# RG-LRU and the front of HGRN2 moved from the mixer tiles into the projection pass of a hybrid encoder layer

## The chip, the cores and the metric

One Trainium2 chip, one core of it. The time is that of one execution of the whole program on the device, in microseconds; the median of three runs is given. The kernel is written at the level of engines: TensorE (PE), VectorE (DVE), ScalarE (ACT), GpSimd (POOL) and SyncE (SP) each run a program of their own in order, and wait for each other on semaphores.

## The reference

One layer, for two groups of tokens that share the weights: a prompt of 2048 and a sample of 32. `D_MODEL` is 1024. A projection to 6536 columns feeds four mixers of width 512; their outputs are gated, joined (2048) and projected back; then comes cross-attention into 256 memory tokens.

```python
h = rms_norm(x, g_pre[l])
p = jnp.matmul(h, w_in[l]).astype(f32)
xa, ga, pb, gb, xbc, dtr, z, qd, fd, idd, gd = split_last(p, SPLITS)
# RG-LRU
xa_c, nca = causal_conv(xa, conv_a[l], lru_conv_w[l], lru_conv_b[l])
...
r = jax.nn.sigmoid(jnp.einsum('btnd,nde->btne', xb, w_r).reshape(Bsz, T, C) + b_r)
i = jax.nn.sigmoid(jnp.einsum('btnd,nde->btne', xb, w_i).reshape(Bsz, T, C) + b_i)
log_a = -LRU_C * r * jax.nn.softplus(-lam)
a = jnp.exp(log_a)
u = jnp.sqrt(-jnp.expm1(2.0 * log_a)) * (i * x)
...
_, h = lax.associative_scan(combine, (a, u), axis=1)
...
ya = ya * jax.nn.silu(ga)
# HGRN2, in chunks of 64
logf = jnp.logaddexp(jnp.log(lb), jnp.log1p(-lb) + jax.nn.log_sigmoid(fd))
...
k = -jnp.expm1(logf)
b = jnp.cumsum(lfc, axis=1)
o = jnp.einsum('blhk,bhkv->blhv', qc * jnp.exp(b), S)
dec = jnp.exp(jnp.where(mask, b[:, :, None] - b[:, None, :], -jnp.inf))
att = jnp.einsum('bthk,bshk,btshk->btsh', qc, kc, dec)
```

With `DEPTH` = 1 the lower bound `lb` is 0, so `logf` is the log-sigmoid of `fd`. The other two mixers are RWKV-7 and Mamba-2 SSD.

## The kernel before

The program is a row of passes, each a block of five engine programs.

`project_pass` normalises and transposes x (one tile of 128 tokens after the other), and then computes the projection, transposed: channels on partitions, tokens (2048 + 32 = 2080) along the free axis. A unit is 128 channels; there are 52 units, in the order of the list `units`, and each has five groups of N = 416 columns. A group is 24 matmuls in a PSUM bank (three per 128 rows of `D_MODEL`, from the split of float32 into a high and a low part). The five groups use banks 0 to 4, so a bank is wanted again five groups later; TensorE waits for that on `bank_free`. Per group ScalarE and VectorE take the bank over: a gate is `tanh` and a product (`silu`), a convolution is ScalarE's column of the newest tap and three taps on VectorE (`own_column`, `older_columns`), a shift is one tap, the rest a copy (`plain`). A unit's 2080 columns are gathered in one of two tiles `out` and stored as one row of `pc` in HBM. On SyncE a unit's weights (512 KB) are loaded when the unit two before is done; VectorE splits them (`split`) at group 2 of the unit before.

`memory_pass` prepares the cross-attention.

`mixer_pass` runs twice: `mixp` over the prompt in 16 tiles of 128 tokens, `mixs` over the sample's 32 tokens in one tile. A tile loads its columns of `pc`: `load_in` (inputs of the convolution, shift and SSD) and `load` (gates, the inputs of HGRN2, and `dt_in` last). Its work is in two halves, written out by hand on each engine. The front (functions `front_...`) prepares a tile: LRU gates on TensorE (`front_gates`), the whole RG-LRU, HGRN2's forget logs, sums and scaled keys and queries, the decays of RWKV-7, and all of SSD. The body of tile i holds the inverses by doubling (`q_level`, `tu_level` of 2 to 32 on TensorE, `qi_level` on VectorE, `level` on ScalarE), the states and outputs of RWKV-7 and HGRN2, and the steps of the front of tile i + 1, put between the levels in a fixed order. Every step has a name in `STEPS` and raises its engine's semaphore; a step waits for names. The order on VectorE that matters here is: `qi_level(4)`; dt, LRU gates, LRU inputs, `front_up`; `qi_level(8)`; `front_one_less`, `front_decays`; `qi_level(16)`; dt; `qi_level(32)`; HGRN states; `front_rwkv`; rhs and sa copies, with `front_rwkv_keys`, `front_seg` and `front_lru` between; `front_scores`, `front_x`, `front_hgrn`; `yb_centred`; `front_ssd`, `front_hgrn_queries`; the outputs. For the first tile of a pass the front runs alone, ahead of the loop. SyncE stores a tile's outputs to `yt`, waits for that store, and then issues `load(i + 2)`.

ScalarE's functions sit in table sets: Tanh, Exp and Square in one, Ln with Exp in another, and a switch is an instruction of its own (`ACT_TABLE_LOAD`). `load_ln_and_exp` puts one in by hand.

After the mixers, `attend_pass` finishes the sample, and `out_pass` and `cross_pass` the prompt; the change touches none of them. All instructions of the mixer's engines are issued by a few helpers, so the profile shows them under the helpers' lines (L1326 TensorE, L1692 to L1706 VectorE, L1152 and L1155 ScalarE, L1079 GpSimd), and they are told apart by their tiles.

## Time and profile before

| | |
|---|---|
| time, median of 3 runs (us) | 3911.25 (3907.21 to 3912.49) |
| the profiled execution, time / span (us) | 3911.24 / 3909.5 |
| busy: PE, PEld, DVE, ACT, POOL (us) | 3277.0, 2857.6, 1740.1, 842.3, 436.1 |
| the same as shares of the span | 84%, 73%, 45%, 22%, 11% |
| mean granted clock of TensorE | 0.92 |
| HBM read / written (MB) | 181.26 / 116.42 |
| normalisation and transposes (us from the start) | 0 to 123.6 |
| projection products | 123.6 to 1334.5 |
| memory pass | 1340 to 1560 |
| mixer, prompt (`mixp`) | 1561 to 2897 |
| mixer, sample (`mixs`) | 2909 to 3018 |
| the rest (sample's attention, output, cross-attention) | 3027 to 3909.5 |

The span is the time from the first instruction to the last. The page's 40 slices give the same picture: TensorE is busy nine tenths in the projection, seven to eight tenths in the mixer, where VectorE stands at six to seven tenths. "Idle before" of a row is how long the engine stood still right before it, and the arrow names who released it.

### The profile page before, as it was taken

Reading aid. Unit: us, or ns where it says so; the run is one execution under the profiler, and the core shown is the slowest. Engines: PE = TensorE matmul, PEld = TensorE weight load, DVE = VectorE, ACT = ScalarE, POOL = GpSimd, SP = SyncE. Lnnn points to the kernel's source line nnn. Section 1 sums busy time; section 2 is a strip of 40 time slices with the busy share of each in tenths; the row PEclk is TensorE's granted clock in tenths of the full one; section 3 lists DMA queues with packets and bytes.
Section 4 is the critical chain, followed back from the end, with each engine's and each line's share of the span. In section 5 each row is a group of like instructions: output and inputs, shape, how many; then the busy total and the mean of one; then the engine's idle time right before and its main releaser. Section 6 shows DMA issues by size and latency. Waiting matters only on the chain. (4 is left out here: it accounts for less than half of the span.)

```text
span 3909.5 us, 74300 instructions
## 1 busy us (share of the span) xinstructions
PE 3277.0 (84%) x31226; PEld 2857.6 (73%) x31226; DVE 1740.1 (45%) x2869; ACT 842.3 (22%) x1687; POOL 436.1 (11%) x493
## 2 busy tenths in 40 slices
PE   2899999998999888577787777777745699979998
PEld 2799999998999755466676666666644188867887
DVE  4333222451222123677767777677723142325443
ACT  2111111120000000333334333343312121121111
POOL 3100000000000001322232222322220000000000
PEclk9999999999999999688888988889875899989999
DMA  3121112118112443311131112311135133341111
GB/s 86 34 81 66 65 65 81 65 65 66 65 65 75 146 162 138 88 47 48 47 88 53 47 48 59 81 48 47 32 58 169 41 107 118 123 173 53 64 64 54
DMA packets 336326, 301.53 MB, mean 77 GB/s; under 512 B 73440, under 2 KB 296672, under 8 KB 329536
## 3 DMA queue, kind: packets, MB, share of 16 engines
q1 hardware_dynamic: 310592, 280.33, 24.5%
q0 software_dynamic: 4608, 16.78, 1.1%
q8 instruction: 203, 3.33, 0.4%
q10 hardware_dynamic: 20864, 0.61, 0.3%
q14 instruction: 59, 0.48, 0.0%
HBM read 181.26 MB, written 116.42 MB: 76 GB/s over the span
## 5 line engine op out<-in xcount | busy, mean ns | idle before, releaser
L536 PE MATMUL in_ps<-in_hT_high,in_w_high 128*128 128x420 f32 x2080 | 737.3, 354 | 18.7 <-DVE in_w_low L411 12.2
L536 PE MATMUL in_ps<-in_hT_high,in_w_low 128*128 128x420 f32 x2080 | 736.1, 354 | 0.0
L536 PE MATMUL in_ps<-in_hT_low,in_w_high 128*128 128x420 f32 x2080 | 735.9, 354 | 0.0
L536 PEld LDWEIGHTS in_ps<-in_hT_high,in_w_high 128*128 128x128 f32 x2080 | 392.5, 189 | 25.7 <-issue 19.1
L536 PEld LDWEIGHTS in_ps<-in_hT_high,in_w_low 128*128 128x128 f32 x2080 | 392.4, 189 | 7.6
L536 PEld LDWEIGHTS in_ps<-in_hT_low,in_w_high 128*128 128x128 f32 x2080 | 392.0, 188 | 7.0
L460 DVE SCALAR_TENSOR_TENSOR in_out<-in_th,in_ps 128x416 f32<-128x416 f32 x100 | 58.5, 587 | 344.4 <-ACT in_th L358 344.4
L358 ACT ACTIVATE in_th<-in_ps 128x416 f32<-128x416 f32 x100 | 51.9, 519 | 576.9 <-PE in_ps L536 576.9
L2660 PE MATMUL mixo_ps<-mixo_w_high,mixo_y_high 128*128 128x512 f32 x512 | 158.7, 391 | 17.4 <-DVE mixo_w_low L2636 17.4
L2660 PE MATMUL mixo_ps<-mixo_w_high,mixo_y_low 128*128 128x512 f32 x512 | 158.3, 391 | 0.0
L2660 PE MATMUL mixo_ps<-mixo_w_low,mixo_y_high 128*128 128x512 f32 x512 | 158.0, 390 | 0.0
L1326 PE MATMUL mixp_ps<-mixp_tu_inv,mixp_lev 64*64 64x64 f32 x2560 | 105.0, 233 | 39.5 <-POOL mixp_lev L1079 29.1
L1326 PE MATMUL mixp_ps<-mixp_qi,mixp_tu_inv 64*64 64x64 f32 x2048 | 93.9, 234 | 50.7 <-DVE mixp_qi L1692 50.6
L2158 POOL MEMSET mem_eps<- 128x1 f32 x1 | 0.1, 99 | 1219.5 <-POOLq L167 1219.5
L1326 PEld LDWEIGHTS mixp_ps<-mixp_tu_inv,mixp_lev 64*64 64x64 f32 x2560 | 93.5, 146 | 58.1 <-issue 55.3
L464 DVE SCALAR_TENSOR_TENSOR in_out<-in_ps,in_conv_w,in_out 128x416 f32<-128x416 f32 (+1 forms) x150 | 96.5, 643 | 79.8 <-ACT in_out L378 76.6
L1155 ACT ACTIVATE mixp_tu_inv<-mixp_ps 128x512 f32<-128x512 f32 (+1 forms) x160 | 87.6, 552 | 191.2 <-PE mixp_ps L1326 190.7
L2660 PEld LDWEIGHTS mixo_ps<-mixo_w_high,mixo_y_high 128*128 128x128 f32 x512 | 96.5, 189 | 38.3 <-issue 18.2
L1326 PEld LDWEIGHTS mixp_ps<-mixp_qi,mixp_tu_inv 64*64 64x64 f32 x2048 | 80.0, 147 | 56.8 <-issue 54.2
L464 DVE SCALAR_TENSOR_TENSOR in_out<-in_ps,in_mu,in_out 128x416 f32<-128x416 f32 (+1 forms) x65 | 41.9, 644 | 177.6 <-ACT in_out L375 177.1
L1692 DVE TENSOR_TENSOR mixp_qi<-mixp_ps,mixp_eye 128x256 f32<-128x256 f32 x160 | 64.8, 420 | 122.9 <-PE mixp_ps L1326 121.6
L2878 PE MATMUL att_ps<-att_qk_high,att_hT_high 128*128 128x512 f32 x256 | 103.1, 403 | 16.6 <-DVE att_hT_low L2818 10.5
(674 smaller groups left out, 6412.7 us busy)
## 6 DMA issues: line engine op xcount, KB each, us to landing
pc<-in_out SPq DMA_DIRECT2D x51, 1040.0 KB, 4.9
in_w_tile<-in_w_in_dram SPq DMA_DIRECT2D x52, 512.0 KB, 3.9
mixp_gate_io<-pc SPq DMA_DIRECT2D x64, 256.0 KB, 3.8
yt<-mixp_gate_io SPq DMA_DIRECT2D x16, 1024.0 KB, 5.9
mixo_y_in<-yt SPq DMA_DIRECT2D x16, 1024.0 KB, 6.0
mixp_xm<-pc SPq DMA_DIRECT2D x16, 832.0 KB, 6.2
mixp_hg_in<-pc SPq DMA_DIRECT2D x16, 768.0 KB, 5.8
in_x_in<-in_x_prompt_dram SPq DMA_DIRECT2D x16, 512.0 KB, 3.2
```

The source lines that it names most:

```text
L358: act.activation(th[n % 3][:, :], ps[:, g, LEAD:LEAD + N], ACT.Tanh, scale=0.5).then_inc(act_took, 1)
L460: vec.scalar_tensor_tensor(dst(u, g), th[silu_at[u, g] % 3][:, :], 1.0, ps[:, g, LEAD:LEAD + N], ADD, MUL).then_inc(bank_free, 1)
L464: ins = vec.scalar_tensor_tensor(o, x, w, o, MUL, ADD)
L536: last = pe.matmul(o, left(a, k), right(b, k), start=p is passes[0], stop=p is passes[-1])
L1155: act.activation(o, x, fn, scale=scale, **k).then_inc(*a_s.did(name))
L1326: return pe.matmul(o, a, b, start=start, stop=stop)
L1692: vec.tensor_tensor(o, a, b, op).then_inc(*steps.did(name))
L2158: link(pool.memset(eps[:, :], NORM_EPS))
L2660: last = pe.matmul(ps[:, 2 * j + half, :], y[j][:, k, :], w[:, k, cols], start=k == 0 and y is y_high and w is w_high, stop=k == YT - 1 an ...
L2878: last = pe.matmul(ps[:, bank + half, :], a[:, k, :], b[:, k, cols], start=k == 0 and a is left[0] and b is high[w], stop=k == KT - 1 and ...
```

## The change

The tiles of `out` become seven tiles of 416 columns (`outs`), and each group is stored for itself (208 KB). RG-LRU is computed in `project_pass`, group by group: item m (20 of them, four channel blocks by five groups) has three stages, spread over following groups of columns (`lru_stages`). Its output goes straight to `yt`. HGRN2's forget logs, cumulative sums and scaled keys and queries are computed there as well, for all 2080 columns of a block of channels; the order of units has the gate GD before the queries QD. The results (`HK2`, `HQ2`, `HQ`, `HK`) go into rows of `pc` (two of them into those of XA and GA, which are free now), and the ends of the chunks into a small tensor `h_ends`. Weights, biases, the softplus of lambda and the sample's LRU state are loaded and prepared in `project_pass`. The first 10 units of TensorE's program are written out, the rest stay a loop.

The mixer loses these steps on all engines, and loads the results. Its `load` has 4 + 4 + 4 rows of gates, 8 + 12 rows for HGRN2, `ends` and `dt_in` (seven transfers, 32 blocks of 64 KB; before six, 28 blocks); `load_in` has 19 blocks (before 23), the store 12 (before 16).

```diff
+HK2, HQ2, HQ, HK = XA, GA, QD, FD
...
-        units += [("conv", XA + t), ("silu", GA + t)]
+        units += [("conv", XA + t), ("gate", GA + t)]
...
-        units += [("raw", FD + t), ("silu", QD + t), ("silu", GD + t), ("raw", ID + t)]
+        units += [("forget", FD + t), ("silu", GD + t), ("query", QD + t), ("raw", ID + t)]
...
+    LRU_FIRST, LRU_ITEMS = GROUPS * 2, 4 * GROUPS
+
+    def lru_stages(u, g):
+
+        ago = GROUPS * u + g - LRU_FIRST
+        stages = ((2, ago // 2 - 1), (0, ago // 2)) if ago % 2 == 0 else ((1, ago // 2),)
+        return [(stage, m) for stage, m in stages if 0 <= m < LRU_ITEMS]
...
+        vectors = [(lru_b[:, 0, :], col(a["lru_b_r"])), (lru_b[:, 1, :], col(a["lru_b_i"])), (lam[:, :], col(a["lru_lambda"])),
+                   (lru_h0[:, :], lru_h_of(state_in)), (conv_b[:, 0:4], col(a["lru_conv_b"])), (conv_b[:, 4:10], col(a["ssd_conv_b"])), (mu[:, :], col(a["rwkv_mu"]))]
...
+            for u, g in SLOTS:
+                if g == 0 and 0 < u < UNITS - 1:
+                    sync.wait_ge(group_done, GROUPS * u)
+                    load_w(u + 1)
+                if (u, g) != SLOTS[0]:
+                    stores_of(*SLOTS[GROUPS * u + g - 1])
...
+            act.wait_ge(lru_w_clear, 1)
+            for dst, src in lru_blocks:
+                act.dma_start(dst, src).then_inc(lru_w_in, 16)
             load_ln_and_exp(nc, act)
...
+            def lru_tanhs(m):
+
+                t = m // GROUPS
+                at_least(act, lru_u, m)
+                act.wait_ge(lru_gated, m + 1)
+                for k, o in enumerate((lru_r, lru_i)):
+                    act.activation(o[:, :], ps[:, 5 + k, 0:N], ACT.Tanh, scale=0.5, bias=lru_b[:, k, t:t + 1]).then_inc(lru_tanh, 1)
+
+            def lru_decays(m):
+
+                act.wait_ge(lru_s, m + 1)
+                at_least(act, lru_y, m)
+                act.activation(lru_a[:, :], lru_r[:, :], ACT.Exp, scale=-1.0).then_inc(lru_decay, 1)
+                act.activation(lru_th[:, :], lru_r[:, :], ACT.Tanh).then_inc(lru_decay, 1)
+                act.wait_ge(lru_decay, 3 * m + 1)
+                act.activation(lru_a2[:, :], lru_a[:, :], ACT.Square).then_inc(lru_decay, 1)
+
+            def lru_roots(m):
+
+                act.wait_ge(lru_less, 2 * m + 2)
+                load_ln_and_exp(nc, act)
+                act.activation(lru_th[:, :], lru_th[:, :], ACT.Ln).then_inc(lru_root, 1)
+                act.wait_ge(lru_root, 2 * m + 1)
+                act.activation(lru_th[:, :], lru_th[:, :], ACT.Exp, scale=0.5).then_inc(lru_root, 1)
...
+            log1p(vec, link, sp[:, 0, :], sp[:, 1, :], sp[:, 2, :], sp[:, 3, :], sp[:, 4, :])
+            link(vec.tensor_scalar(sp[:, 3, :], sp[:, 3, :], LRU_C / 2, None, MUL))
             vec.sem_inc(vectors_made, 1)
...
+            def lru_inputs(m):
+
+                t, g = m // GROUPS, m % GROUPS
+                vec.wait_ge(lru_tanh, 2 * m + 2)
+                vec.tensor_scalar(lru_r[:, :], lru_r[:, :], 1.0, sp[:, 3, t:t + 1], ADD, MUL).then_inc(lru_s, 1)
+                vec.scalar_tensor_tensor(lru_i[:, :], lru_i[:, :], 1.0, cv[:, g * N:(g + 1) * N], ADD, MUL).then_inc(lru_ix, 1)
...
+                vec.tensor_tensor_scan(h[:, 0:m0], lru_a[:, 0:m0], lru_th[:, 0:m0], before[:, N - 1:N] if g else 0.0, MUL, ADD).then_inc(lru_scanned, 1)
...
+                vec.scalar_tensor_tensor(h_logf[:, cols], ps[:, g, LEAD:LEAD + N], 0.0, f_ln[g % 2][:, :], ALU.min, SUBTRACT).then_inc(hg_log, 1)
+                vec.wait_ge(hg_log, GROUPS * t + g + 1)
+                vec.tensor_tensor(h_logk[:, cols], h_logf[:, cols], ps[:, g, LEAD:LEAD + N], SUBTRACT).then_inc(bank_free, 1)
...
+                vec.tensor_tensor_scan(h_cum[:, cols], first[:, ph:ph + N], h_logf[:, cols],
...
+            def lru_gates(m):
+
+                t, g = m // GROUPS, m % GROUPS
+                pe.wait_ge(bank_free, freed(unit_of[XA + t], g))
+                at_least(pe, lru_tanh, 2 * m)
+                for k in range(2):
+                    last = pe.matmul(ps[:, 5 + k, 0:N], lru_w[:, k, t, :], cv[:, g * N:(g + 1) * N], start=True, stop=True)
+                last.then_inc(lru_gated, 1)
...
-                for dst, t, n in ((cv[j][:, :, :], XA, 4), (xm[j][:, :, :], PB, 13), (xbc[j][:, :, :], XBC, 6)):
+                for dst, t, n in ((xm[j][:, :, :], PB, 13), (xbc[j][:, :, :], XBC, 6)):
...
+                for dst, t, n in ((gate_io[j][:, 0:4, :], GB, 4), (gate_io[j][:, 4:8, :], Z, 4), (gate_io[j][:, 8:12, :], GD, 4),
+                                  (hg_in[j][:, 0:8, :], HK2, 8), (hg_in[j][:, 8:20, :], QD, 12)):
...
+                chunks = h_ends[:, :, bass.ds(i * NCH + t_first // 64, NCH), :].rearrange("q p c b -> p q c b")
+                sync.dma_start(ends[j][:, :, :, :], chunks).then_inc(loaded[j], 16)
...
                 if more:
                     in_ready(vec, jn, nn)
                     ready(vec, jn, nn)
                     front_dt_input(jn)
-                    front_lru_gates()
                     front_inputs(jn)
-                    front_lru_inputs(jn)
                     front_up()
                 qi_level(8)
                 if more:
-                    front_one_less()
                     front_decays(jn)
...
-                    if more and k == NCH - 1:
-                        front_lru(jn)
...
                     front_x(jn)
-                    front_hgrn(jn)
...
                     front_ssd(jn)
-                    front_hgrn_queries(jn)
```

ScalarE loses the same steps in the mixer (`front_lru`, `front_lru_decay`, `front_hgrn`, and the logs and roots of both), TensorE `front_gates`. TensorE's wait for a tile's loads now stands before the attention products of HGRN2 instead of before its keys.

## Rows read from the trace of the kernel before

**Rows 1.** busy time by stage: the steady mixer tiles, then the projection products
```profile
1640.80:2841.10 1200.30, 928.14 (x18735) 801.74 (x18733) 865.36 (x1636) 453.29 (x825) 313.50 (x255) 0.88 0.20 55
123.60:1334.50 1210.90, 1198.72 (x6257) 1176.88 (x6257) 339.08 (x533) 145.02 (x292) 0.00 (x0) 0.99 0.25 66
```

**Rows 2.** PE in order of time in one steady tile (start us, us, what, idle before)
```profile
2209.43 2.05 PE L1326 MATMUL mixp_ps<-mixp_cv,mixp_lru_w 128*128 128x128 f32 x16
2225.37 1.12 PE L1326 MATMUL mixp_ps<-mixp_qi,mixp_tu_inv 64*64 64x64 f32 x16 [2.56 <-DVE mixp_qi L1692]
2251.15 0.63 PE L1412 MATMUL mixp_ps<-mixp_ident,mixp_xbc 128*128 128x128 f32 x4 [1.05 <-DVE mixp_dts L1692]
2261.35 1.38 PE L1326 MATMUL mixp_ps<-mixp_yb,mixp_headmean 128*128 128x512 f32 x2 [2.84 <-POOL mixp_yb L1079]
```

**Rows 3.** DVE in the same tile
```profile
2209.08 0.89 DVE L1692 TENSOR_TENSOR mixp_qi<-mixp_ps,mixp_eye 128x256 f32<-128x256 f32 x2 [2.75 <-PE mixp_ps L1326]
2218.72 0.74 DVE L1692 TENSOR_TENSOR mixp_qi<-mixp_ps,mixp_eye 128x256 f32<-128x256 f32 x2
2219.38 0.68 DVE L1692 TENSOR_TENSOR mixp_ls<-mixp_la 128x512 f32<-128x512 f32 x1
2224.81 0.75 DVE L1692 TENSOR_TENSOR mixp_qi<-mixp_ps,mixp_eye 128x256 f32<-128x256 f32 x2
2254.97 0.68 DVE L1698 SCALAR_TENSOR_TENSOR mixp_logf<-mixp_hg_in,mixp_logf 128x512 f32<-128x512 f32 x1
2259.40 0.68 DVE L1692 TENSOR_TENSOR mixp_yb<-mixp_yb,mixp_ps 128x512 f32<-128x512 f32 x1
2270.01 0.69 DVE L1692 TENSOR_TENSOR mixp_yb<-mixp_yb 128x512 f32<-128x512 f32 x1 [2.13 <-ACT mixp_yd L1155]
```

**Rows 4.** ACT in the same tile
```profile
2212.60 0.63 ACT L1152 ACTIVATE mixp_fe<-mixp_hg_in 128x512 f32<-128x512 f32 x1 [2.90 <-DMA mixp_dt_in<-dtr]
2222.01 1.28 ACT L1152 ACT_TABLE_LOAD   x1
```

**Rows 5.** busy time, granted clock and DMA in two stretches of that tile
```profile
2209.00:2216.00 7.00, 6.90 (x112) 5.75 (x109) 2.68 (x6) 4.04 (x10) 1.70 (x2) 1.00 0.98 260
2225.00:2232.00 7.00, 6.63 (x127) 6.54 (x129) 2.86 (x13) 3.96 (x7) 0.00 (x0) 0.55 0.00 0
```

**Rows 6.** DMA issues in the mixer (KB each, median us to landing)
```profile
yt<-mixp_gate_io SPq DMA_DIRECT2D x15, 1024.0 KB, 5.9
mixp_dt_in<-dtr SPq DMA_DIRECT2D x14, 4.0 KB, 7.1
```

**Rows 7.** groups of instructions (count, busy us, mean ns, idle before): projection, one mixer scan
```profile
L464 DVE SCALAR_TENSOR_TENSOR in_out<-in_ps,in_conv_w,in_out 128x416 f32<-128x416 f32 (+1 forms) x150 | 96.5, 643 | 79.8 <-ACT in_out L378 76.6
L411 DVE TENSOR_TENSOR in_w_low<-in_w_tile,in_w_high 128x1024 fp32r<-128x1024 f32 x52 | 64.1, 1233 | 1.8
L378 ACT ACTIVATE in_out<-in_ps,in_conv_b,in_conv_w 128x416 f32<-128x416 f32 x50 | 35.0, 700 | 169.9 <-PE in_ps L536 169.9
L1706 DVE TENSOR_TENSOR_SCAN mixp_hcum<-mixp_first,mixp_logf 128x512 f32<-128x512 f32 x16 | 19.5, 1216 | 0.0
```

**Rows 8.** PE in the memory stage, 64 records of 32 f32 products
```profile
1354.73 27.73 PE L2230 MATMUL mem_ps<-mem_w_half,mem_memT 128*128 128x512 f32 x64 [1.31 <-DVE mem_memT L2194]
```

**Rows 9.** the start, ACT's DMA issues and first work
```profile
17.33 0.57 ACTq L330 DMA_DIRECT2D in_edge<-in_state_lru_conv_dram  x1
18.49 1.28 ACT L92 ACT_TABLE_LOAD   x1 [18.49 <-issue]
```

**Rows 10.** the start of the prompt mixer
```profile
1566.05 1.03 ACTq L1144 DMA_DIRECT2D mixp_lru_w<-in_lru_w_r_dram  x1
1583.04 0.17 DVE L1671 TENSOR_SCALAR mixp_sp<-mixp_sp 128x4 f32<-128x4 f32 x1 [28.10 <-POOLq L1074]
1599.14 0.42 DVE L1695 TENSOR_SCALAR mixp_wa<-mixp_wa 128x512 f32<-128x512 f32 x1
```

**Rows 11.** the sample mixer's gate products
```profile
2932.81 3.59 PE L1326 MATMUL mixs_ps<-mixs_cv,mixs_lru_w 128*128 128x32 f32 x16 [1.50 <-DVEq L1685]
```

More of the change, by code:

```diff
@@ L162, in project_pass @@
[L162 to L165 removed]
+    has_tanh = ("silu", "gate", "query")
+    SLOTS = [(u, g) for u in range(UNITS) for g in range(GROUPS)]
+    freed = lambda u, g: GROUPS * (u + 1) + g + 1
+    taken, tanh_at, xbc_at, out_at, edge_before = {}, {}, {}, {}, {}
+    n_taken, n_stored, edge_units = 0, [0] * OUTS, []
@@ new lines, in project_pass @@
+    for u, g in SLOTS:
+        kind, n = units[u]
+        if kind in has_edges:
+            n_taken += 4 if g == GROUPS - 1 else 1
+            if g == 0:
+                edge_units.append(u)
+        elif kind != "dt" and kind != "raw":
+            n_taken += 3 if kind == "forget" else 1
+        taken[u, g] = n_taken
+        if kind in has_tanh:
+            tanh_at[u, g] = len(tanh_at)
+        if kind == "conv_silu":
+            xbc_at[u, g] = len(xbc_at)
+        outs = {"dt": (), "conv": (), "forget": (), "query": ("hq", "hq2")}.get(kind, ("out",))
+        for name in outs:
+            r = len(out_at) % OUTS
+            out_at[name, u, g] = (r, n_stored[r])
+            n_stored[r] += 32 if kind == "gate" and g == GROUPS - 1 else 16
@@ new lines, in _ @@
+            for u, g in SLOTS:
+                kind, n = units[u]
+                if kind in has_tanh:
+                    tanh(u, g)
+                elif kind == "forget":
+                    forget(u, g)
+                elif kind in has_edges:
+                    own_column(u, g)
+                if kind == "conv_silu" and g:
+                    conv_tanh(u, g - 1)
+                if kind == "conv_silu" and g == GROUPS - 1:
+                    conv_tanh(u, g)
+                for stage, m in lru_stages(u, g):
+                    if stage == 0:
+                        lru_tanhs(m)
+                    elif stage == 1:
+                        lru_decays(m)
+                    else:
+                        lru_roots(m)
+                if units[u - 1][0] == "forget" and g == 2:
+                    hgrn_exps(units[u - 1][1] - FD)
@@ new lines, in _ @@
+            for u, g in SLOTS:
+                kind, n = units[u]
+                if (u, g) == (2, 0):
+                    vec.wait_ge(dt_turned, 1)
+                    vec.tensor_copy(dt_out[:, :, :].rearrange("p t h -> p (t h)"), ps[:, 7, 0:(NT + 1) * HEADS]).then_inc(dt_copied, 1)
+                if g == 2 and 0 < u < UNITS - 1:
+                    split(u + 1)
+                if kind in ("raw", "dt"):
+                    plain(u, g)
+                elif kind in ("silu", "gate"):
+                    silu(u, g)
+                elif kind == "forget":
+                    forget(u, g)
+                elif kind == "query":
+                    query(u, g)
+                else:
+                    older_columns(u, g)
+                if kind == "conv_silu" and g:
+                    conv_silu(u, g - 1)
+                if kind == "conv_silu" and g == GROUPS - 1:
+                    conv_silu(u, g)
+                for stage, m in lru_stages(u, g):
+                    if stage == 0:
+                        lru_inputs(m)
+                    elif stage == 1:
+                        lru_one_less(m)
+                    else:
+                        lru_output(m)
+                if units[u - 1][0] == "forget":
+                    if g == 0:
+                        hgrn_spans(units[u - 1][1] - FD)
+                    if g == 1:
+                        hgrn_rel(units[u - 1][1] - FD)
+                    if g == GROUPS - 1:
+                        hgrn_keys(units[u - 1][1] - FD)
@@ L552, in _ @@
-            last.then_inc(dt_turned, 1)
-            with pe.Fori(1, UNITS // 2) as i:
+                    group(u, u % 2, g)
+                    for stage, m in lru_stages(u, g):
+                        if stage == 0:
+                            lru_gates(m)
+                if u == 1:
+                    turn_dt()
+            with pe.Fori(UNROLLED // 2, UNITS // 2) as i:
                 for j in range(2):
-                    products(2 * i + j, j)
+                    pe.wait_ge(w_split_made, 2 * i + j + 1)
+                    for g in range(GROUPS):
+                        group(2 * i + j, j, g)
@@ L1987, in body @@
                 vec.wait_ge(*pe_s.at("h_kv"))
[L1988 removed]
+                e2 = ends[j]
                 for k in range(NCH):
```

636 lines of the change are left out of this document (332 added, 304 removed).

## The prediction

> **What bounds the kernel now.** I read the busy time by stage first. The projection products last 1210.9 us and TensorE is busy in 1198.72 of them; VectorE works 339 us there and ScalarE 145 [rows 1]. That stage is bound by TensorE, with room on the two engines that are to get new work. The fifteen steady mixer tiles last 1200.3 us, 80.0 us each, and nothing is saturated: TensorE 928, VectorE 865 [rows 1]. So I read one tile in order of time on three engines. It is a chain that changes hands. TensorE idles 2.56 us before the `tu16` products, because the VectorE copy `qi16` stands behind the front's work (2224.81) [rows 2, 3]; 1.05 us before the transposes of x, behind the RG-LRU scan and its neighbours; and 2.84 us before the variance product, because `yb_centred` starts only at 2259.40, after HGRN steps that began at 2254.97 [rows 2, 3]. Near the end VectorE itself waits, 2.13 us, for ScalarE's roots [rows 3]. And at 2212.60 ScalarE had waited 2.90 us for the tile's loads [rows 4]. Idle time that a removal exposes elsewhere is no gain, so I price the change by the stretches of this chain and not by VectorE's busy time.
>
> **The projection (costs).** (1) Gate products: 20 items of two float32 products over 416 columns. In the memory stage 32 float32 products over 512 columns take 27.73 us, 0.867 each [rows 8]; times 416/512 that is 0.704, and 40 of them are +28.2 us. TensorE is the bound here, so all of it is on the path. Bounds: 27, and 36 if each pair also empties the pipeline. (2) Start: ScalarE's queue issues eight more transfers (four vectors, four blocks of gate weights) before its first table load at 18.49, and that load is what the first tile waits for. A vector costs 0.57 [rows 9], a block 1.03 [rows 10]; 4 x 0.57 + 4 x about 0.8 = +5.5 (4.6 to 8). (3) The softplus chain of lambda moves from the mixers to the point between the weight splits and the first product: two small ScalarE and nine small dependent VectorE steps, some 0.2 us each as in the mixer's own prologue (0.17 at 1583.04 [rows 10]), +2.3 (1.5 to 3). (4) Does the new elementwise work hide? Take two groups of columns, one LRU item. TensorE needs 2 x 4.66 (1210.9/260) + 1.41 = 10.7 us. VectorE, in the fullest place (conv units): six taps and six LRU operations at no more than 0.643, a scan of 1.216 x 416/512 = 0.99, and two fifths of a split at most 2 x 1.23: 9.7 us [rows 7]. ScalarE: nine operations at no more than 0.70 [rows 7] and two table loads of 1.28 [rows 4]: 8.9. Both fit, and a group's bank is wanted again only five groups (some 20 us) later, so I take 0; below zero is excluded, since no product leaves this stage. The HGRN units are easier: three or four operations a group, and per four units three full-width ones on VectorE, at most 5 x 0.643 = 3.2 us each, against 93 us of products. Waits added on queues: SyncE's load of the next weights now stands behind stores that wait for VectorE group by group; it is wanted two groups later, when the split comes, and the slack is that of the banks. VectorE and ScalarE wait for a store of seven tiles ago; behind such a wait stands the freeing of a bank, again five groups deep. (5) Stores of 208 KB instead of 1040 KB, five times as many: the DMA share was 0.25 [rows 1], so 0. Sum +36 (33 to 47).
>
> ScalarE's loads of tables deserve a second look. In the trace the table load at 2222.01 takes 1.28 us and the engine goes on at once [rows 4], so 48 switches in the projection cost at most 62 us of an engine with over 1000 us free. The Trainium skill ("ScalarE: Activation LUTs", What ACT_TABLE_LOAD costs) says that a switch also drains the pipeline and costs about 2.66 us in all, and its rule is to batch by table set, which this change breaks: 20 items switch twice. By that figure an item would take ScalarE 8.9 + 2.8 = 11.7 us against 10.7, and the sum would be 20 us higher, about -38. The trace doesn't show the drain; the matching rival is F.
>
> **The prologues (gains).** Prompt mixer: VectorE starts at 1583.04 and reaches `log_w` at 1599.14 [rows 10], 16.1 us. Without the lambda chain, the gate products, the biased copy and the LRU scaling there remain some 8.3 us (small sets, dt, a table load and the tanh of wl, the up product and its copy, the tanh of wa), and GpSimd is 1 us sooner without the memset of gate weights: -8.8. Behind it the LRU scan block goes, -3; the HGRN block was under TensorE's products. -12 (-8 to -16). Sample mixer: gate products of 3.59 us [rows 11], four fewer transfers ahead of the states, and short operations: -7 (-4 to -10).
>
> **A steady tile (gains).** Stretch by stretch, with its landing times.
> Until `qi4` (2209.08) nothing changes. From there the gate products, 2.05 us at 2209.43, go [rows 2], but the load is late: ScalarE and VectorE can't begin the next front before 2212.60 [rows 4]. What the change does to that load: 32 blocks of 64 KB instead of 28, at the 260 GB/s of that stretch [rows 5], +1.0; a yt store of 768 KB instead of 1024 KB before it (5.9 us [rows 6]), about -0.7; and a new transfer of 512 pieces of 16 bytes, issued ahead of dt_in. No such transfer is in the trace. The nearest is dt_in, 4 KB, landing 7.1 us after its issue [rows 6], behind a full queue; between 0 and 3 us, I take 1.2. The load lands 1.5 us later, 2214.1. Then dt, tanh of wl, the copies of `tu4`, `up`, `q8`: `qi8` starts at 2217.9 instead of 2218.72, gain 0.8.
> From `qi8` to `qi16` the three `one_less` operations go, 2219.38 to 2221.16, 1.8 us [rows 3], but the tanh of wa becomes the late one for 0.5: gain 1.3, together 2.1. TensorE's idle of 2.56 shrinks to about 1.4.
> From `qi16` to the HGRN states ScalarE loses three operations (1.7 us), but TensorE, at a granted clock of 0.55 in 2225 to 2232 [rows 5], is late by itself: 0. From there to the second `sa` all is as before.
> Then the LRU block goes (3 us) and 4.4 us of HGRN between 2254.97 and 2259.40 [rows 3]. What is late next: the transposes wait for TensorE (it gives 1.15 of it), then `yb_mean` at about 2254.4, then the SSD products, which end 2.8 us earlier than they are used now. So `yc`, GpSimd's square, the norm product, ScalarE's roots and `yb_normed` (2270.01, where VectorE waits already [rows 3]) come 2.7 us earlier, not 7.4. The HGRN queries (2.4 us) lay beside a wait of 2.13.
> Sum 4.8, and with some of the clock loss back 5.0 us a tile (of some 22 us of VectorE time); x 15 = -75. Bounds: 2.7 alone (load as late as 3 us more) to 8.
>
> The clock: TensorE ran at 1.2 GHz (0.55 on average) right after the thinly used stretch before 2225, and at 2.4 GHz while it was dense [rows 5]. A shorter gap could keep it up; half of 6.6 us of work would be some 3 us a tile.
>
> **Rivals.** A: as above, -58 (span 3851.5). B: the clock stays up and VectorE was later than I see: 9 us a tile, -135 + 17 = -118, 3792 us of time. For it: the 2.56 us wait goes nearly away. Against: the stretch behind it waits for ScalarE's table loads too. C: the load takes the place of the front: every tile waits 3 us more than I have it, 2 us a tile remain: -30 + 17 = -13, 3898. For it: 0.98 of DMA busy in 2209 to 2216 [rows 5] and a wait of 2.90 already. D, on the slow side: the projection. LRU's stages alternate ScalarE, VectorE and TensorE in strict order, and margins are 9.7 and 8.9 against 10.7. If in-order waits add 4 us to each item beyond the banks' slack, 20 x 4 = 80: -58 + 80 = +22, 3933 us. It decides from 58/20 = 2.9 us an item on. Against it: the buffers are five banks and seven tiles deep, and each stage is asked for two groups later. E: the moves cancel: C with the projection's upper end of 47, -30 + 28 = -2, 3909. F: in the 20 items a switch of tables costs ScalarE as long again as its row, 2 x 1.28 more: 8.9 + 2.6 = 11.5 against 10.7, +16, 3869 us. For it only the bound of 0.70 for each operation; against it the row, after which the next operation starts at once.
>
> **How the numbers follow.** The profiled execution took 3911.24 us, its span 3909.5; the median of three is 3911.25, so nothing separates them. 36 - 12 - 7 - 75 = -58: 3853. Chances: A 0.52 (3825 to 3882), B 0.15, C 0.14, D 0.09, E 0.04, F 0.03, and 0.03 for more than B. The range 3785 to 3904 takes in A, B, C and F and leaves D, E and the far end. About 0.2% is what can be told from no change: faster by more 0.86 (A, B, F, nearly all of C, the far end), within it 0.05, slower 0.09.
>
> **What the profile after would show.** Projection products 28 us longer with TensorE idle below 20 us (right) or with idle before products that names VectorE or ScalarE (D). Tile period near 75 us; near 71 with a clock above 0.93 (B); near 78 with ScalarE and VectorE waiting on dt_in or the chunk ends (C). The wait before `tu16` near 1.4, that before the variance product under 1. First projection product at 131 instead of 123.6. I am wrong most likely in the load's landing and in how the clock answers.

## The result and the profile after

| | before | after |
|---|---|---|
| time, median (us) | 3910.68 | 3845.86 (3839.79 to 3853.11) |
| ratio to the kernel before | | 0.9836, 95% interval 0.9817 to 0.9855 |
| the profiled execution: span (us) | 3909.5 | 3851.0 |
| busy: PE, PEld, DVE, ACT, POOL (us) | 3277.0, 2857.6, 1740.1, 842.3, 436.1 | 3263.7, 2833.8, 1664.4, 919.3, 431.2 |
| mean granted clock of TensorE | 0.92 | 0.93 |

The forecast was 3853, and the total came out 7 us below it. The parts did not come out so well. The profiled execution is the slowest of the four runs, so its stretches hold 58.5 of the 65 us between the medians; where the other 6 lie isn't known. Here is the profiled execution cut at the same five events in both kernels (first projection product, first product of the memory pass, first and last `bonus_v` of the prompt's mixer, end):

| stretch (us) | before | after | difference | forecast |
|---|---|---|---|---|
| up to the first projection product | 123.6 | 130.5 | +6.9 | +7.8 |
| projection, up to the first memory product | 1231.1 | 1280.5 | +49.4 | +28.2 |
| memory pass and the mixer's prologue | 286.0 | 277.8 | -8.3 | -12 |
| 15 steady tiles | 1200.3 | 1109.0 | -91.3 | -75 |
| last tile, sample mixer, the rest | 1068.5 | 1053.3 | -15.2 | -7 |
| sum | 3909.5 | 3851.0 | -58.5 | -58.0 |

The projection lost 21 us more than forecast; the tiles and what follows them gained 24 more. The sum hides both. By stage (busy time of PE, PEld, DVE, ACT, POOL, then granted clock, DMA share, GB/s), answering [rows 1]:

```profile
1688.70:2797.80 1109.10, 889.57 (x18495) 768.74 (x18495) 643.75 (x1231) 358.03 (x646) 308.98 (x255) 0.90 0.21 55
130.50:1392.20 1261.70, 1225.53 (x6336) 1191.14 (x6337) 506.28 (x797) 329.48 (x579) 0.00 (x0) 0.99 0.29 68
```

A tile lasts 73.9 us instead of 80.0, and VectorE is busy in 58% of it instead of 72%. In the projection TensorE is idle 36 us. The list of waits (total, times, longest) shows that this is one wait, and that it was there before, at a third of its size. After, then before:

```profile
DVE in_w_high L610 <- DMA in_w_tile<-in_w_in_dram: 46.5, 1, 46.5
PE in_ps L874 <- DVE in_w_low L612: 36.2, 1, 36.2
```

```profile
DVE in_w_high L409 <- DMA in_w_tile<-in_w_in_dram: 22.6, 1, 22.6
PE in_ps L536 <- DVE in_w_low L411: 12.2, 1, 12.2
```

Who holds up the weights is seen in SyncE's queue in order of time (start, length, what, count). After:

```profile
895.90 0.39 SPq L319 DMA_DIRECT2D in_w_tile<-in_w_in_dram  x1
900.00 6.72 SPq L338 DMA_DIRECT2D pc<-in_outs  x4
906.83 0.38 SPq L390 DMA_DIRECT2D out_dram<-in_lru_last  x1
907.26 12.59 SPq L392 DMA_DIRECT2D out_dram<-in_edge_out  x7
920.20 6.94 SPq L390 DMA_DIRECT2D out_dram<-in_lru_last  x1
927.18 27.88 SPq L392 DMA_DIRECT2D out_dram<-in_edge_out  x7
955.10 2.44 SPq L338 DMA_DIRECT2D pc<-in_outs  x2
957.59 0.43 SPq L319 DMA_DIRECT2D in_w_tile<-in_w_in_dram  x1
```

and before:

```profile
884.10 0.37 SPq L254 DMA_DIRECT2D in_w_tile<-in_w_in_dram  x1
885.33 0.35 SPq L274 DMA_DIRECT2D pc<-in_out  x1
885.73 10.31 SPq L290 DMA_DIRECT2D out_dram<-in_edge_p  x7
896.08 25.69 SPq L290 DMA_DIRECT2D out_dram<-in_edge  x7
921.81 4.42 SPq L254 DMA_DIRECT2D in_w_tile<-in_w_in_dram  x1
```

Sixteen small stores (the convolutions' edges, the shift's, and now RG-LRU's last state; 2 to 6.5 KB each) take 48 us to issue. The view of DMA for 906 to 960 us of the kernel after shows what goes on meanwhile: all 16 DMA engines are busy, and move next to nothing, in pieces of 4 bytes.

```profile
DMA  0798999999999999999999999999999999999999
DMA packets 12378, 0.32 MB, mean 6 GB/s; under 512 B 12220, under 2 KB 12377, under 8 KB 12377
```

Before, these stores were issued 1.6 us behind a weight load (884.10, 885.73), with a whole unit of five groups to go until the next. Now they come two groups of columns later (not three, as the expectation below has it), 10.9 us behind the weight load (895.90, 906.83), there are two more of them, and the next weight load waits behind all. From one weight load to the next SyncE's queue takes 61.7 us instead of 37.7. Of these 24.0 us more, 9.3 are the later place, 7.4 the two new stores, 4.8 the longer issue of the fourteen others, and 2.5 two group stores that now stand behind them.

### The profile page after: what moved, and what is told of

The parts are those of the page before. It is cut to its first block and busy times, and to the rows that moved or that the text cites. A ratio compares the mean times of both kernels' runs of the same rounds, so it can differ in the third digit from the quotient of the medians.

```text
span 3851.0 us, 73942 instructions
## 1 busy us (share of the span) xinstructions
PE 3263.7 (85%) x31034; PEld 2833.8 (74%) x31034; DVE 1664.4 (43%) x2665; ACT 919.3 (24%) x1766; POOL 431.2 (11%) x496
## 3 DMA queue, kind: packets, MB, share of 16 engines
q1 hardware_dynamic: 334640, 280.60, 25.9%
## 5 line engine op out<-in xcount | busy, mean ns | idle before, releaser
L677 DVE SCALAR_TENSOR_TENSOR in_outs<-in_th,in_ps 128x416 f32<-128x416 f32 x100 | 58.6, 587 | 232.1 <-ACT in_th L482 227.9
L1626 PE MATMUL mixp_ps<-mixp_tu_inv,mixp_qi 64*64 64x64 f32 x2560 | 107.6, 221 | 13.3 <-issue 11.2
L2855 PEld LDWEIGHTS mixo_ps<-mixo_w_high,mixo_y_low 128*128 128x128 f32 x512 | 96.7, 189 | 20.3
L2855 PEld LDWEIGHTS mixo_ps<-mixo_w_low,mixo_y_high 128*128 128x128 f32 x512 | 96.7, 189 | 20.3
```

The source lines that it names most:

```text
L677: vec.scalar_tensor_tensor(dst[:, :], th[tanh_at[u, g] % THS][:, :], 1.0, ps[:, g, LEAD:LEAD + N], ADD, MUL).then_inc(bank_free, 1)
L1626: return pe.matmul(o, a, b, start=start, stop=stop)
L2855: last = pe.matmul(ps[:, 2 * j + half, :], y[j][:, k, :], w[:, k, cols], start=k == 0 and y is y_high and w is w_high, stop=k == YT - 1 an ...
```

## The steady tile, step by step

Starts on VectorE, in us after the tile's `bonus_v`, each the mean of the fifteen tiles, worked out from VectorE's rows:

| step | before | after | gained so far |
|---|---|---|---|
| dt's first use (the load has landed) | 10.8 | 11.0 | -0.1 |
| biased copy of `up` | 17.3 | 16.2 | 1.1 |
| scan of the decays | 21.3 | 19.0 | 2.3 |
| first HGRN state | 31.9 | 28.9 | 3.0 |
| `seg` | 43.3 | 40.4 | 2.9 |
| SSD scores | 51.3 | 46.8 | 4.5 |
| `yb_centred` | 59.5 | 51.9 | 7.6 |
| `yb_normed` | 70.1 | 63.9 | 6.2 |
| next `bonus_v` | 80.0 | 73.9 | 6.1 |

The waits of TensorE in the fifteen tiles, some of the largest after and then before, answer [rows 2]; last the row of the `tu16` products after:

```profile
PE mixp_ps L1626 <- POOL mixp_yc L1414: 48.5, 15, 3.2
PE mixp_ps L1626 <- DVE mixp_rhs L1983: 43.6, 15, 2.9
PE mixp_ps L1626 <- DVE mixp_qi L1974: 29.0, 33, 1.3
```

```profile
PE mixp_ps L1326 <- DVE mixp_qi L1692: 50.5, 30, 2.6
PE mixp_ps L1326 <- POOL mixp_yb L1079: 40.5, 15, 2.9
PE mixp_ps L1326 <- POOL mixp_yc L1079: 27.9, 15, 2.3
PE mixp_ps L1412 <- DVE mixp_dts L1692: 12.5, 12, 1.0
```

```profile
2228.62 0.68 PE L1626 MATMUL mixp_ps<-mixp_qi,mixp_tu_inv 64*64 64x64 f32 x16 [1.33 <-DVE mixp_qi L1974]
```

The wait for `qi` fell from 3.4 to 1.9 us a tile, the one before `tu16` from 2.56 to 1.33 (the prediction's sign for being right was 1.4), that for the variance product (`yb`) from 2.7 to nothing; half of the latter came back as a longer wait for `yc`, the SSD output, which is what is late now. The wait for `rhs` did not change (43.6 us in the fifteen tiles, 44.7 before). VectorE shows the same: it waits 2.33 us for TensorE before `yc`, and 4.09 for ScalarE's roots where [rows 3] had 2.13.

```profile
2257.24 0.69 DVE L1974 TENSOR_TENSOR mixp_yb<-mixp_yb,mixp_ps 128x512 f32<-128x512 f32 x1 [1.57 <-PE mixp_ps L1626]
2260.26 0.69 DVE L1974 TENSOR_TENSOR mixp_yc<-mixp_ps,mixp_e_acs 128x512 f32<-128x512 f32 x1 [2.33 <-PE mixp_ps L1626]
2269.18 0.69 DVE L1974 TENSOR_TENSOR mixp_yb<-mixp_yb 128x512 f32<-128x512 f32 x1 [4.09 <-ACT mixp_yd L1486]
```

## Experiments

The runs were made on four occasions, each beside the kernel before (medians 3917.4, 3912.3, 3910.0 and 3910.9). Totals are compared by their ratio to it; stretches come from one profiled execution each.

### The state stores, spread out

```diff
-                    for k, s in enumerate(states_out):
-                        sync.dma_start(lru_h_of(s), lru_last[:, k, :]).then_inc(lru_stored, 16)
-                        for src, dst in edge_views(s, lambda r0, r1, m: edge_out[:, r0:r1, k, m]):
-                            sync.dma_start(dst, src).then_inc(edges_stored, 16)
+                if g == 2 and 0 <= u - last_edge - 1 < len(late):
+                    dst, src, semaphore = late[u - last_edge - 1]
+                    sync.dma_start(dst, src).then_inc(semaphore, 16)
```

> The changed kernel, with SyncE's 16 scattered state stores issued one per unit (units 32 to 47, at group 2) instead of all in a row between two loads of weights. Theory (SyncE held the next weight load behind 48 us of issues, and the change moved these issues three groups closer to that load and added two): TensorE's one wait of 36.2 us for the weight split goes, and with it some 2 us at half clock: 3846 - 38 = 3808 us (3803 to 3814), projection products 1262 - 38 = 1224 us. Rival (the stores are slow wherever they stand, because 4-byte pieces fill the DMA engines, and each one holds back the group stores and through them the banks): the wait is cut into pieces, total above 3826 us.

> The kernel before, with its 14 scattered state stores issued one per unit in the same way. Theory: its one wait of 12.2 us for the weight split goes, with 3 us at half clock: 3911 - 15 = 3896 us (3892 to 3900). With both kernels free of this stall the projection products differ by the gate products alone: 20 items of about 1.33 us (two groups last 10.5 us with an item and 9.17 without) = 27 us (25 to 29), as forecast (+28.2), and not by the 51 us seen. Rival (in-order waits of the new elementwise work cost the rest, and the stall covers it only by chance): the difference stays above 35 us.

Measured: the kernel after 0.9745 (0.9728 to 0.9762) instead of 0.9836, so 36 us less; the kernel before 0.9934 (0.9917 to 0.9952), 26 us less (19 to 33), more than the 15 expected. Its profile is 13.5 us shorter than that of the kernel before, with 14.7 less in the projection (1231.1 to 1216.4 us); the rest of the 26 it doesn't show. In the kernel after that stretch is 1241.9 instead of 1280.5, 38.6 less (counted to the last projection product it is 1223.5, where 1224 was expected). No wait of TensorE for a weight split is left in either. The stall was one of issue order, and the stores show no cost when each has a unit's time. Between the two kernels without it the projection differs by 25.5 us, 1.28 for each of the 20 items: that is the price of the gate products, and the elementwise work adds nothing that can be told from it. The rest of the 49.4 us, 24, is the stall's growth. The stall's length varies: 29.2 to 43.5 us (mean 34) in the nine profiles of kernels with this order of issue, 12.2 and 17.7 us in the two with the order of before. So its growth is 24 us in the pair that was compared, and some 19 by the means.

### RG-LRU's last state, not stored by the mixers

The kernel after gained 8 us more than forecast behind the last tile. At each end of a mixer pass its state stores land in 2 us, where the kernel before has 9 (KB, us from issue to landing). Before, then after:

```profile
out_dram<-mixp_turn SPq DMA_DIRECT2D x4, 64.0 KB, 9.2
out_dram<-mixp_hg_s SPq DMA_DIRECT2D x1, 128.0 KB, 10.4
out_dram<-mixp_lru_h SPq DMA_DIRECT2D x1, 2.0 KB, 10.2
```

```profile
out_dram<-mixp_turn SPq DMA_DIRECT2D x4, 64.0 KB, 2.2
out_dram<-mixp_hg_s SPq DMA_DIRECT2D x1, 128.0 KB, 2.0
```

So, in the kernel before (whose output then lacks that state):

```diff
-            out = [(src, dst) for dst, src in state_views(state_out)]
+            out = [(src, dst) for dst, src in state_views(state_out)[1:]]
```

> The kernel before, with RG-LRU's last state (2 KB in 512 pieces of 4 bytes) not stored at the end of the two mixer passes; it is left out of the output. In the kernel before the other state stores (64 and 128 KB) land 9.2 to 10.4 us after their issue at both places, in the changed kernel, where this store stands in the projection, 2.0 to 2.2. Theory (the small pieces hold up the stores behind them, and the next pass waits for all): from the last issue to the next pass 8.5 us become 2.0, twice, and one issue less: -13 to -14 us, 3911 - 14 = 3897 (3893 to 3900), ratio 0.9965. Rival (the states wait for something else at a pass's end, as the store of yt or the write to HBM itself, and the changed kernel is sooner there for other reasons): less than 4 us, ratio above 0.999.

Measured: 0.9966 (0.9953 to 0.9979), 13.3 us less (8 to 18). The other stores land in 2.0 and 2.2 us at both ends, and the next pass starts 2.0 us behind the last issue instead of 8.5:

```profile
2899.52 0.37 SPq L1053 DMA_DIRECT2D out_dram<-mixp_hg_s  x1
2899.94 2.71 SPq L1053 DMA_DIRECT2D out_dram<-mixp_turn  x4
2904.62 0.41 SPq L995 DMA_DIRECT2D mixs_cv<-pc  x1
```

The theory holds: 512 pieces of 4 bytes hold up the 384 KB behind them by 7 to 8 us, twice. Of the 15.2 us that the change gained behind the start of its last tile, 11 to 13 are this: by the profiles that stretch is 11.0 us shorter without the store (1068.5 to 1057.4).

So 2 to 4 us are left for all the rest, and the forecast had 7 for the sample's mixer alone. That pass did not become shorter. The queue of SyncE shows it, from the pass's first load to the store of its output, 102.4 us before and 102.3 after:

```profile
2908.70 0.41 SPq L995 DMA_DIRECT2D mixs_cv<-pc  x1
3011.14 0.36 SPq L1022 DMA_DIRECT2D yt<-mixs_gate_io  x1
```

```profile
2855.42 0.40 SPq L1331 DMA_DIRECT2D mixs_xm<-pc  x1
2957.69 0.36 SPq L1359 DMA_DIRECT2D yt<-mixs_gate_io  x1
```

In four more profiles of kernels with the changed mixer it is 101.4 to 102.8. From VectorE's first operation to `bonus_v` the pass gained 3.7 us (42.6 to 38.9), but from there to the HGRN states it lost 4.7 (11.95 to 16.65), with TensorE's granted clock at 0.59 in that stretch instead of 0.78. No run separates the cause.

### The small loads of the start, and both repairs together

```diff
+            for t in range(2, NT):
+                sync.wait_ge(normed, t)
+                load_x(t, t % 2)
+                for dst, src, semaphore in small[2 * t - 4:2 * t - 2]:
+                    sync.dma_start(dst, src).then_inc(semaphore, 16)
...
-            for dst, src in vectors:
-                act.dma_start(dst, src).then_inc(vectors_in, 16)
...
             split(0)
+            vec.sem_inc(bank_free, GROUPS)
             split(1)
```

> The changed kernel, with the 26 small loads of vectors, edges and gate weights issued by SyncE, two behind each load of x, instead of by ScalarE ahead of its first work; and the banks are released after the first weight split, ahead of the second split and of lambda's chain. Theory: ScalarE's first work waits for x instead, about 7 us from the start instead of 23.2, so the first transposes come 15 us sooner (17 at most); the first product another 4 to 5 us sooner (second split 1.9, small steps 0.8, chain 2.2): first product at 130.5 - 20 = 111 (108 to 115), total 3846 - 20 = 3826 us (3822 to 3831). Rival (the x tiles themselves are late, or SyncE's issues of small loads hold back the loads of x): the stage up to the first product loses less than 10 us.

> The changed kernel with both repairs: the state stores one per unit, and the 26 small loads issued by SyncE behind the loads of x with the banks released after the first weight split. Theory: the two are in different places and add up, since the part of the start's gain that was given back (the stall at the state stores was 43.5 us instead of 36.2 there) has no place left: first product at 107.5, products 1242 us as in the run with spread stores, ratio to the kernel before 0.9745 - 23/3917 = 0.9686, some 3788 us for a kernel before at 3911. Rival (what is won at the start is waited for elsewhere, as the weights of the second unit come late): ratio above 0.972.

The start alone: 0.9802 (0.9784 to 0.9821). ScalarE's first table load stands at 0.8 instead of 23.20 (18.49 in [rows 9]), the first transposes at 8.28 instead of 27.04, the first product at 107.51 instead of 130.49: 23 us, 3 more than expected. The stall at the state stores was 43.5 us in this run, 7.3 longer, and the total shows 13 (give or take 10). The run changes two things, the loads' issue and the place where the banks are released; by the rows 18.8 us come ahead of the first transposes and 4.2 behind.

Both together: 0.9683 (0.9667 to 0.9699), 3786.8 us beside 3848.0 for the changed kernel on the same chip. First product at 107.38, projection 1242.6 us. They add up as expected, and this kernel is faster than both that were given.

```profile
5.60 1.06 ACT L454 ACTIVATE in_junk<-in_x_in 128x1024 f32<-128x1024 f32 x1 [3.51 <-DMA in_x_in<-in_x_prompt_dram]
```

In the run with both, ScalarE's first work waits for x itself; TensorE's last 4.5 us before the first product are a wait for the first weight split, which stands behind the last normalisation.

### Two more table switches in each LRU item

```diff
                 load_ln_and_exp(nc, act)
+                load_tanh(nc, act)
+                load_ln_and_exp(nc, act)
```

> The changed kernel, with two more switches of ScalarE's table in each of the 20 LRU items of the projection (Exp's and Tanh's set and back to Ln's, ahead of the roots). In the changed kernel an item lasts 10.5 us, TensorE is never idle in it, and ScalarE stands idle some 3.2 us of it in two waits. Theory (a switch costs its row, 1.28 us, and no more): 2.56 us more per item fit into that idle time, the time stays within 5 us of the changed kernel (ratio to the kernel before 0.983 to 0.986). Rival F (a switch costs as long again as its row, four switches 10.2 us an item instead of 5.1 for the two now plus 2.6): ScalarE needs some 12.4 us for a 10.5 us item, 2 us x 20 = +40 us, with TensorE waiting for banks in units 2 to 9.

Measured: 0.9869 (0.9840 to 0.9897), 13 us more than the kernel after (give or take 14; 7 by the profiled executions). In the row of each switch and the one behind it nothing but 1.28 us is seen:

```profile
254.13 1.28 ACT L93 ACT_TABLE_LOAD   x1 [0.66 <-DVE in_lru_th L732]
255.42 1.28 ACT L99 ACT_TABLE_LOAD   x1
256.70 1.28 ACT L93 ACT_TABLE_LOAD   x1
258.00 0.55 ACT L554 ACTIVATE in_lru_th<-in_lru_th 128x416 f32<-128x416 f32 x1
258.58 0.55 ACT L556 ACTIVATE in_lru_th<-in_lru_th 128x416 f32<-128x416 f32 x1
259.15 1.28 ACT L537 ACT_TABLE_LOAD   x1
260.45 0.61 ACT L537 ACTIVATE in_lru_r<-in_ps,in_lru_b 128x416 f32<-128x416 f32 x1
```

The Trainium skill ("ScalarE: Activation LUTs", What ACT_TABLE_LOAD costs) adds a drain of about 1.38 us to each switch; the trace does not show one. The operation behind the third load starts 0.02 us after it, and the load at 259.15, which stands right behind a working operation, starts 0.02 us after that one's end and is followed as closely. F's price (40 us here) is refuted. But "within 5 us" missed too: the projection lasts 1293.3 us, 12.8 more, although its stall at the state stores is 4 us shorter. TensorE, which never waits in the LRU items of the kernel after, now does. The wait, and busy time in 190 to 390 us of this kernel, then of the kernel after:

```profile
PE in_ps L896 <- ACT in_lru_i L537: 9.2, 6, 2.1
```

```profile
190.00:390.00 200.00, 190.78 (x911) 172.85 (x910) 122.93 (x213) 168.71 (x234) 0.00 (x0) 0.97 0.13 38
```

```profile
190.00:390.00 200.00, 200.00 (x985) 184.89 (x984) 135.39 (x229) 138.31 (x217) 0.00 (x0) 1.00 0.14 43
```

ScalarE is busy 84% there, not full. Its 3.2 us of idle time in an item were not all cover: the stages of an item follow each other across three engines, and a longer one on ScalarE delays the next gate products before ScalarE is full. Of 2.56 us more an item, 0.8 are paid (16.8 us over 20 items: 12.8, and the 4 of the shorter stall) and 1.7 hidden. So D's mechanism is real and stood some 1.7 us an item away.

### Where the load of a tile lands

```diff
                 if more:
+                    load_small(i + 2, j)
                     sync.wait_ge(stored, i * 16 + 16)
```

> The changed kernel, with the two small loads of a mixer tile (chunk ends in 16-byte pieces, and dt_in) issued right after the tile's store instead of behind the five large loads. Theory: dt_in lands last, some 2 us behind the large loads (at 2218.7 for large loads issued by 2210.6 that land in 5.7 to 6.7 us), and starts ScalarE and VectorE on the next front; earlier by 1.5 to 2 us, of which TensorE's levels hide a part: 0.7 to 1.5 us a tile, 3846 - 16 = 3830 us (3822 to 3837). Rival (the front is not what is late between the second and third level, TensorE's own products are): within 4 us of 3846, although the loads land sooner.

> The changed kernel, with the two small loads issued ahead of the large ones and on a semaphore of their own: ScalarE and VectorE wait for these alone before the next front, and for the large loads only before front_ssd, which uses their gate. Moving the small loads alone left dt's first use at 10.73 us after bonus_v (10.95 before), since the large ones now landed last. Theory (the landing of the large loads holds back the front): dt and the tanh of wl start as soon as VectorE and ScalarE are free, 1 to 2 us earlier, the up product and all behind it too: -1.2 us a tile (-0.7 to -2), 3846 - 19 = 3827 us on the first chip, ratio 0.979. Rival (the up product waits for TensorE's own levels, whose copies come from ScalarE): less than 0.3 us a tile, ratio 0.982 to 0.985.

Measured: 0.9847 (0.9824 to 0.9871) and 0.9834 (0.9806 to 0.9862), both the same as the kernel after. With the small loads first, HGRN2's large one lands 8.4 us after its issue, the ends and dt after 3.9 and 2.9 (6.7, 6.0 and 4.3 in the kernel after). And when the front needn't wait for it, dt's first use moves from 11.0 to 10.5 us, and the period, 73.7, stays within those of kernels with the same mixer (73.7 to 74.6): VectorE comes from `qi4` at that time, and `up` waits for TensorE's levels. My theory fell: in the kernel after the landing of the loads is not on the path. For the kernel before no run tests it. There VectorE went from the landing (2212.60 in the tile of [rows 3]) through the LRU gates and inputs to `up` (2217.58), with waits for ScalarE alone (0.34 and 1.60 us), so the landing may have been on the path.

### The two VectorE blocks, put back as empty work

```diff
+                        bstt(spare[0][:, :, :], ones, 0.5, ones, MUL, MUL, "x_lru0")
+                        bown()
+                        bscan(spare[1][:, :, :], ones, spare[0][:, :, :], "x_lru1")
+                        bown()
+                        bstt(spare[0][:, :, :], spare[1][:, :, :], 0.5, ones, MUL, MUL, "x_lru2")
```

and likewise six operations ahead of `yb_centred` for HGRN's.

> The changed kernel, with work of the length of RG-LRU's block put back on VectorE in each tile of the prompt's mixer, at its old place (one product, one scan of 1.2 us, one product, 2.9 us in all; the data are nobody's). Theory (the chain changes hands; VectorE waits 1.35 us for TensorE right behind this place, so that much is cover): 2.9 - 1.35 = +1.5 us a tile, the period from 74 to 75.5, 16 tiles +25 us; the whole forecast of the last stretch is of this kind. Rival (in a stretch where VectorE works without a gap, each us of it counts): +2.9 us a tile, +46 us.

> The changed kernel, with work of the length of HGRN's block (4.2 us: five operations of full width, a scan among them, and a small copy) put back on VectorE at its old place, ahead of yb_centred. Theory: VectorE waits 1.57 us for TensorE before yb_centred now, so that step comes 2.6 us later; from there to yb_normed there are 11.9 us now and 10.6 in the kernel before, so 1.3 us of the 2.6 are lost again in waits: +1.3 us a tile (1.0 to 2.0), +21 us in all; with the LRU block it makes up the 3.3 us that this stretch gained. Rival (full price beyond the first wait): +2.6 us a tile, +42 us; or the full length of 4.2, +67 us.

> The changed kernel with both blocks of VectorE work put back in each tile of the prompt's mixer (2.9 us and 4.2 us). One at a time they cost 0.7 and 1.1 us of the stretch from seg to yb_normed (24.15 and 24.56 instead of 23.48), 1.8 in sum, against the 3.3 us that this stretch gained by the change (26.79 to 23.48). Theory (the waits for TensorE in this stretch, 1.35, 1.57 and 2.33 us, are one cover and can be used only once): both together cost more than their sum, 2.8 us of the stretch (26.3), period up by 2.2 to 3.3 us. Rival (the blocks cost 1.8 together, and the other 1.5 us came from something else that left, HGRN's queries or ScalarE's work): 25.3 for the stretch, period up by 1 to 1.8 us.

> The changed kernel itself, beside the other two on their chip, as their base: ratio 0.9836 to the kernel before (0.982 to 0.9855), tile period 73.9 us (73.5 to 74.6, as in the runs whose mixer is the same), the one wait for weights of 36 us.

| kernel | ratio (interval) | period (us) | `seg` to `yb_normed` (us) |
|---|---|---|---|
| after, again | 0.9836 (0.9818 to 0.9854) | 74.3 | 23.5 |
| + LRU block, 2.9 us | 0.9867 (0.9837 to 0.9897) | 74.9 | 24.1 |
| + HGRN block, 4.2 us | 0.9895 (0.9863 to 0.9927) | 74.4 | 24.5 |
| + both | 0.9975 (0.9963 to 0.9987) | 76.7 | 25.9 |
| before | 1 | 80.0 | 26.8 |

Profiles of kernels with the mixer unchanged have periods of 73.7 to 74.6 us. By the periods one block alone costs next to nothing, by the stretch 0.6 and 1.0 us, by the totals 12 and 23 us, each give or take 14. The sizes expected for one block (25 and 21 us) are too high by the profiles, and not excluded by the totals; the rivals' full prices (46 and 42 or 67) are. In the HGRN run VectorE runs through where it waited before:

```profile
2257.63 0.68 DVE L1975 TENSOR_TENSOR mixp_yb<-mixp_yb,mixp_ps 128x512 f32<-128x512 f32 x1
2258.23 0.68 DVE L1975 TENSOR_TENSOR mixp_yc<-mixp_ps,mixp_e_acs 128x512 f32<-128x512 f32 x1
```

The 4.2 us were paid for the most part out of the waits of 1.57 and 2.33 us. Both together cost 51 us in total beside the kernel after on the same chip (54 by the ratios), 2.4 a tile by the periods and 2.4 in the stretch (expected 2.2 to 3.3, and 2.8; the rival had 1.8). In the stretch, which differs by no more than 0.3 us between profiles of kernels with the same mixer, that is more than the two apart (1.6 to 1.7), and so it is by the periods; the totals (12 and 23 against 51) are too wide to tell. So the waits are one cover, used once. Sixteen tiles at 2.4 us are 39 of the 51 us; the profiles place 6 more outside the tiles, and the rest not at all. These 2.4 are the two blocks' part of the 6.1 us of a tile, and of the 3.3 that the stretch gained. What else left it (HGRN's queries, ScalarE's operations) was not put back; that it holds the rest is not shown.

## Why the prediction was right, and where only its sum was

**Gate products.** Forecast 28.2 us, measured 25.5. The mechanism was right; the 0.704 us a product was scaled from wider products, and the difference gives 0.64.

**Start.** Forecast +5.5 and +2.3; ScalarE's first table load moved by 4.7 (23.20 against 18.49 of [rows 9]), the first product by 2.2 more.

**Elementwise work in the projection.** Forecast 0, and none is seen: in the LRU items TensorE never waits. D did not happen, with some 1.7 us an item to spare on ScalarE.

**The step that failed** is that on SyncE's queue: "SyncE's load of the next weights now stands behind stores that wait for VectorE group by group". I priced the group stores that the change added, and left out the state stores in the same loop, which it moved two groups closer to the next weight load and made two more. A wait of 12.2 us in the trace of before, ended by a weight split, said that this queue had no slack at one place. It cost 24 us (19 by the means). The spread kernels show it. By the signs that the prediction set for itself, the projection failed: 49.4 us longer and 36 idle, where 28 and below 20 were asked for.

**Prologues.** The prompt's gained 8.3 (forecast 12, bounds 8 to 16; 10.3 on the mean of all profiles). For the sample I had 7 (bounds 4 to 10), and that term was wrong: the pass is 0.2 us shorter, because what it gained up to `bonus_v` was lost again behind. What hides it is a term that the sum lacks, a store that the mixers lost and that I gave no price: RG-LRU's state. By the run without it, 11 to 13 us of the 15.2 that were gained behind the last `bonus_v`.

**Steady tile.** To `qi8` forecast 0.8, measured 1.1 (at `up`). To the decays' scan and `qi16` forecast 1.3 more, measured 1.2. To the HGRN states forecast 0, measured 0.7. From `seg` to `yb_normed` forecast 2.7, measured 3.3. The reading of the chain came out stretch by stretch, also that 22 us of VectorE work would bring 5 or 6 of time. Only the last stretch was tested by putting work back, and in part; for the others the agreement of forecast and profile is all there is. Two details were not right. The load was to land 1.5 us later; dt's first use is 0.1 later, counted from `bonus_v` (at most 0.4 in other profiles), and the two experiments on it show that in the kernel after its landing doesn't matter. So C did not happen. And I gave the clock nothing between `qi16` and the states. The 0.55 of [rows 5] was that of one tile, the second lowest of the fifteen; their mean in the same stretch is 0.85. There, in the two slices of 3 us from 24 to 30 after `bonus_v`, its mean over the tiles went from 0.83 and 0.82 to 0.98 and 1.00, as the idle time ahead of it shrank. That is B's mechanism at a small scale, at most the 0.7 us of this stretch; no run here separates it from the rest.

**The sum** of 58 held by luck, because errors cancelled: +21 in the projection, +4 in the prompt's prologue, -16 in the tiles, -8 behind them, -1 at the start. (B's 3792 should be 3793 by its own terms; nothing rests on it.) With all profiles of the same mixers the period is 74.2 us against 79.8, a gain of 5.6 us a tile rather than 6.1, which is nearer to the forecast of 5.0.

## What to carry to other kernels

Before pricing what a change adds to a queue, list everything that stands in that queue near the place, with its length: sixteen small stores in 4-byte pieces, moved by two groups, cost 24 us where the elementwise work that was moved cost none. Look in the trace of before for single long waits in a stage that is busy 99% of its time; they are invisible in its totals, and one grew here when the order changed. And price a block that leaves a chain by the waits behind it: here 7.1 us of VectorE work were worth 2.4, and either part alone far less than its length.

## What the runs showed of the hardware

A store in 4-byte pieces takes the DMA engines, not the bandwidth: 12220 pieces kept all 16 engines busy for 54 us at 6 GB/s, some 0.07 us of one engine for each, and 512 of them ahead of other stores made those land 7 us later. The Trainium skill ("DMA: Bandwidth & Descriptors", Specifications) gives 512 B as the least size for full rate. The trace agrees as far as it goes, 6 GB/s in 4-byte pieces against 260 in [rows 5]; no run here tries sizes near 512 B.

ScalarE's switch of tables costs its 1.28 us wherever it was seen, 40 of them added or not.

TensorE's clock: with both blocks back it is at 0.50 and 0.53 in the slices from 60 to 66 us after `bonus_v` (below 0.9 in all fifteen tiles), right behind 6 us in which TensorE is busy about half the time. In the kernel after those 6 us are about as thinly used, and the clock is at 0.65 behind them on average, at 0.72 and 0.77 in a second profile. So part of what idle time costs is paid behind it, at 1.2 GHz instead of 2.4; whether the blocks added to that part, no run separates.
